# Sums of weight blocks on VectorE instead of GpSimd, and one ScalarE copy placed later, in a hybrid decoder trunk

## What is computed

```
u = rmsnorm(h) * valid
(a_q, a_f, a_i, a_g, b_qkv, ..., c_gk, c_g, gate_logits) = split(u @ w_in)
y_a = hgrn2(...); y_b = gated_deltanet(...); y_c = gla(...)
gates = sigmoid(gate_logits)                       # 3 x 1024 columns of w_in
merged = sum over the three of gates * (y @ w_branch)
h = h + merged @ w_out
h = h + hier_moe(rmsnorm(h))                       # 32 experts, top 2
out = rmsnorm(h)
```

## Time and profile before

| | |
|---|---|
| time, median of 3 runs | 1096.6 us (1095.65 to 1100.54) |
| the profiled execution's own time | 1095.69 us |
| its span in the trace | 1093.3 us |
| mean granted TensorE clock | 0.981 |
| busy: PE | 1035.0 us (95%) |
| busy: DVE | 528.0 us (48%) |
| busy: ACT | 309.3 us (28%) |
| busy: POOL | 137.4 us (13%) |

### The profile page before, as it was taken

The page is one execution under the profiler, slowest core; times in us unless marked ns, Lnnn a source line. Parts: engine busy times, 40 slices in busy tenths (PEclk is TensorE's granted clock), DMA queues, the critical chain, the costliest instruction groups (busy, mean ns, idle before and its releaser), DMA issues. The chain is left out here.

```text
span 1093.3 us, 20473 instructions
## 1 busy us (share of the span) xinstructions
PE 1035.0 (95%) x8841; PEld 697.7 (64%) x8841; DVE 528.0 (48%) x1026; ACT 309.3 (28%) x573; POOL 137.4 (13%) x121
## 2 busy tenths in 40 slices
PE   9999999998998998998999999999998999878897
PEld 8676676876776776776756556444456665535454
DVE  5766566658458457458454454423235322111114
ACT  3454535343343343243333033010110111001013
POOL 4220202022022022022000000000001222211110
PEclk9999999999999998999999999999999999989899
DMA  9222212240241230331212211154937999999976
GB/s 275 59 59 59 76 43 77 64 97 24 75 82 28 72 82 20 79 74 32 76 44 74 59 58 60 58 201 156 350 136 284 409 414 414 415 417 414 416 318 240
DMA packets 111964, 174.72 MB, mean 160 GB/s; under 512 B 9011, under 2 KB 87100, under 8 KB 103554
## 3 DMA queue, kind: packets, MB, share of 16 engines
q1 hardware_dynamic: 99010, 134.93, 35.7%
q10 hardware_dynamic: 7136, 27.33, 6.3%
q0 software_dynamic: 5728, 11.14, 3.8%
HBM read 169.16 MB, written 12.60 MB: 166 GB/s over the span
## 5 line engine op out<-in xcount | busy, mean ns | idle before, releaser
L791 PE MATMUL ps<-arena 128*128 128x256 f32 x672 | 168.6, 395 | 0.0
L791 PEld LDWEIGHTS ps<-arena 128*128 128x128 f32 x672 | 123.4, 193 | 17.1
L1465 DVE TENSOR_TENSOR arena<-arena 128x256 f32<-128x256 f32 (+6 forms) x198 | 103.5, 565 | 60.0 <-ACT arena L1261 37.0
L824 PE MATMUL ps<-arena 128*128 128x512 f32 x288 | 128.2, 595 | 1.2 <-DVE arena L1804 1.2
L821 PE MATMUL ps<-arena 128*128 128x264 f32 x400 | 123.1, 389 | 0.8 <-DVE gates L1563 0.8
L822 PE MATMUL ps<-arena 128*128 128x264 f32 x400 | 121.7, 386 | 0.0
L2289 PE MATMUL ps<-arena,gates 128*64 128x256 f32 (+1 forms) x1088 | 106.4, 354 | 15.9 <-DMA arena<-in_expert_w_up 15.8
L2289 PEld LDWEIGHTS ps<-arena,gates 128*64 128x64 f32 x1088 | 73.6, 144 | 55.1 <-DMA arena<-in_expert_w_up 24.1
L824 PEld LDWEIGHTS ps<-arena 128*128 128x128 f32 x288 | 53.6, 190 | 62.3 <-issue 61.8
L815 PE MATMUL ps<-yT,arena 128*128 128x512 f32 x192 | 84.8, 596 | 2.1 <-DVE gates L1563 1.4
L822 PEld LDWEIGHTS ps<-arena 128*128 128x128 f32 x400 | 76.0, 190 | 13.0
(11 more groups left out here) (373 smaller groups left out, 1394.5 us busy)
## 6 DMA issues: line engine op xcount, KB each, us to landing
arena<-in_w_in SPq DMA_DIRECT2D x68, 512.0 KB, 3.9
arena<-in_expert_w_gate SPq DMA_DIRECT2D x27, 1024.0 KB
arena<-in_expert_w_up SPq DMA_DIRECT2D x27, 1024.0 KB
arena<-in_expert_w_down ACTq DMA_DIRECT2D x16, 1024.0 KB, 33.4
arena<-in_w_branch SPq DMA_DIRECT2D x12, 512.0 KB, 4.0
arena<-in_expert_w_down SPq DMA_DIRECT2D x6, 1024.0 KB, 17.2
C<-in_expert_w_gate SPq DMA_DIRECT2D x5, 1024.0 KB
gates<-in_expert_w_up SPq DMA_DIRECT2D x5, 1024.0 KB
```

What stands on the lines that cost most here:

```text
L791: mm = t.matmul(dst, wt[:, k, :], rhs[:, k, :], start=(k == 0), stop=(k == KH - 1))
L824: mm = t.matmul(dst, wt, uT[:, k, META:], start=(k == 0), stop=(k == KD - 1))
L1465: v.tensor_tensor(out_, a_, b2, op).then_inc(*q.did(name))
```

## The change

The twelve quadruples of sums go from GpSimd's list to VectorE's, each sum at a place of its own in the round: A's S1 and S2 at level 1 behind the gate product, S4 and S3 at level 2; B's S1, S2 and S4 between `min` and `kn`, and S3 between `less` and `unit` of q; C's S1 at level 1 of B's round, S2 at level 2, S4 and S3 at level 4. The arithmetic and the waits are the same; S3 now waits for S4, and the semaphore `pair_weights` is counted by VectorE. GpSimd keeps the four token mixes of the setup and its transfers. Apart from that, `keep_product` of B stands behind the softplus of the values on ScalarE instead of ahead of it. TensorE's list is the same instruction for instruction.

```diff
-            def mix_weights(stage, r):
-                n, p = pair_block(stage, r), pair_no(stage, r)
...
-                g.tensor_tensor(s1, second[:, 0:KH], second[:, KH:], ALU.add).then_inc(*pair_pool.did(f"S1.{p}"))
...
             mix_tokens()
-            for r in range(A_R - 1):
-                mix_weights("a", r)
...
-                mix_weights("b", r)
-                mix_weights("c", r)
...
                 a.activation(b_n, pair(4), ACT.Copy).then_inc(*b_act.did(f"N.{r}"))
-                keep_product("b", r)
                 a.wait_ge(*b_dve.after(f"v3.{r}"))
                 softplus(b_act, ("abv", "ev", "lv"), r, b_vb[:, 0:TOK], b_s[:, 0:TOK])
+                keep_product("b", r)
                 a.wait_ge(*b_dve.after(f"tv.{r}"))
...
+            def mix_weights(name, stage, r):
+
+                n, p = pair_block(stage, r), pair_no(stage, r)
+                first, second = ring[:, n % RING, :, :], ring[:, (n + 1) % RING, :, :]
+                s1, s2, s4 = (mixed_w[:, m] for m in range(3))
+                if name == "S1":
+                    for m in (n, n + 1):
+                        v.wait_ge(sem(f"block_loaded{m % RING}"), (m // RING + 1) * 16)
+                if name in ("S2", "S4"):
+                    v.wait_ge(*pair_mix.after({"S2": "S1", "S4": "S2"}[name] + f".{p}"))
+                if p and name != "S3":
+                    v.wait_ge(*pair_pe.after({"S1": "P5", "S2": "P6", "S4": "P3"}[name] + f".{p - 1}"))
+                if name == "S3":
+                    v.wait_ge(*pair_mix.after(f"S4.{p}"))
...
+                v.tensor_tensor(out_, a_, b2, op).then_inc(*pair_mix.did(f"{name}.{p}"))
...
                         tt(a_dve, f"g.{r}", a_g, real(0), a_sg)
+                        mix_weights("S1", "a", r)
+                        mix_weights("S2", "a", r)
+                    if l == 2:
+                        mix_weights("S4", "a", r)
+                        mix_weights("S3", "a", r)
...
+                mix_weights("S1", "b", r)
+                mix_weights("S2", "b", r)
+                mix_weights("S4", "b", r)
                 v.wait_ge(*b_act.after(f"rik.{r}"))
                 tt(b_dve, f"kn.{r}", b_kf, b_kf, b_em)
...
                 less("q", b_nw[:, 0:TOK], cq, b_nw[:, 0:TOK], r)
+                mix_weights("S3", "b", r)
                 unit("q", b_qf, cq, b_nw, r)
```

More of the change, by code:

```diff
@@ L540, in hybrid_trunk @@
                       each(C_R - 1, c_finish_names()))
-        pair_pool = Order("pair_weights", [f"{n}.{p}" for p in range(PAIRS) for n in ("S1", "S2", "S4", "S3")])
+        pair_mix = Order("pair_weights", [f"{n}.{p}" for p in range(PAIRS) for n in ("S1", "S2", "S4", "S3")])
         pair_pe = Order("pair_products", [f"{n}.{p}" for p in range(PAIRS) for n in ("P1", "P5", "P6", "P3")])
@@ L684, in mixers_gpsimd @@
             g.wait_ge(sem("rows_sent"), 16)
-            mix_weights("a", A_R - 1)
             rv = rows_dram.rearrange("(t h) (k p) -> k h t p", h=B_R, k=2)
@@ L763, in pair_step @@
                             t.wait_ge(*tokens_mixed.after("T4"))
-                        t.wait_ge(*pair_pool.after(f"S1.{p}"))
+                        t.wait_ge(*pair_mix.after(f"S1.{p}"))
                         if stage == "c":
@@ L769, in pair_step @@
                     if name == "P6":
-                        t.wait_ge(*pair_pool.after(f"S2.{p}"))
+                        t.wait_ge(*pair_mix.after(f"S2.{p}"))
                         t.wait_ge(*pair_copy.after(f"P1.{p}"))
                     if name == "P3":
-                        t.wait_ge(*pair_pool.after(f"S4.{p}"))
+                        t.wait_ge(*pair_mix.after(f"S4.{p}"))
                         if stage == "c":
@@ L778, in pair_step @@
                     if name == "P7":
-                        t.wait_ge(*pair_pool.after(f"S3.{p}"))
+                        t.wait_ge(*pair_mix.after(f"S3.{p}"))
                         t.wait_ge(*pair_sum.after(f"U2.{p}"))
@@ L1523, in c_finish @@
                     tt(c_dve, f"y_{s}.{r}", yT[:, 8 + 2 * r + s, :], c_zz[s], c_g[s])
+            def mix_weights(name, stage, r):
[11 more added lines that the diff above has]
+                    v.wait_ge(*pair_mix.after(f"S4.{p}"))
+                out_, a_, b2, op = {"S1": (s1, second[:, 0:KH], second[:, KH:], ALU.add), "S2": (s2, s1, first[:, 0:KH], ALU.subtract),
+                                    "S4": (s4, first[:, KH:], s2, ALU.subtract),
+                                    "S3": (second[:, 0:KH], first[:, 0:KH], second[:, 0:KH], ALU.subtract)}[name]
+                v.tensor_tensor(out_, a_, b2, op).then_inc(*pair_mix.did(f"{name}.{p}"))
             def gate_second(stage, r):
```

21 lines of the change are left out of this document (6 added, 15 removed).

## The result

The changed kernel takes 1081.68 us (median; 1079.12 to 1082.65) against 1096.12 us for the kernel before in the same comparison: ratio 0.9856, 95% interval 0.9824 to 0.9888. The prediction was 1080, with a range of 1076 to 1086. The profiled execution took 1080.85 us, with a span of 1079.0 us against 1093.3 before.

A forecast was written before the change was run, and what follows sets the result against it. TensorE, 95% busy, was the bound, so other engines count only where it waits, in stage B. 10.7 + 0.9 + 4.9 - 0.1 = 16.4 us gave 1079.3, put at 1080; range 1077 to 1082, with two rivals 1076 to 1086.

The forecast's parts named there:

- The chain to `vT` and `Z1`: Stage B: shorter `Da`, `vm`, `vr` and an earlier logarithm start `Z1` 2.67 us earlier per round, 10.7 us in four.
- rival (3): GpSimd isn't the cause of the long `Da`, `vm`, `vr`; only the copy's 2.4 us remain, 1094 us; chance 0.05.
- The spare time at `vT`: Stage B: the wait of 2.51 us at `vT` goes, with 0.3 us to spare.
- Round 0: Round 0 of B: `less` of k gets 0.94 us shorter, which fits into the waits at `ssk` and `KK`: 0.9 us.
- no cost, no gain: GpSimd's transfers of decay and beta rows keep their place with nothing ahead of them, so the time does not change.
- The clock: Stage B: without the long wait the granted clock does not fall in rounds 0 to 2, 4.9 us, between 0 and 4.9.
- The pause ahead of `kn`: Stage B: three sums of 2.18 us fill VectorE's pause of 2.25 us; 0.1 us lost in all, up to 0.4.
- A's sums: Levels 1 and 2 of A: four sums, about 2.9 us, end 1.3 us before TensorE asks at level 3; no wait.
- C's sums and S3: Stage B: C's sums fit where VectorE waits in the levels, S3's 0.60 us in a pause of 0.71; no cost.
- (1): The clock falls all the same, or at another place; 11.5 us are won, 1085 us; chance 0.10.
- (4): The pauses are too short, since a sum takes VectorE 1.47 to 1.58 us; slower, 1103 us; chance 0.04.
- (2): A wait at P6 or `vT` takes the old one's place; 2 to 4 us less won, 1082 to 1084 us; chance 0.12.

The follow-up runs named there:

- e1: The kernel before with only ScalarE's copy of P1 moved behind the softplus of the values in B, sums left on GpSimd: 1089.77 us, 0.9933 of before.
- e10: The changed kernel with four more VectorE operations between `tv` and `Da` in each round of B: 1096.36 us, 0.9989 of before.
- e7: The changed kernel with ScalarE's root of the keys moved ahead of the two exponentials in B, sums unmoved: 1079.15 us.
- e3: The kernel before with the copy moved and GpSimd's sums for C's pair waiting for VectorE's `qg` of the round: 1081.45 us, 0.9861 of before.
- e2: The changed kernel with the copy of P1 moved back ahead of the softplus, sums on VectorE: 1085.23 us, 0.9898 of before.
- e6: The changed kernel with B's S1, S2 and S4 moved into earlier pauses of VectorE, ScalarE's order unchanged: 1080.58 us.
- e5: The changed kernel with both the keys' root ahead of the exponentials and B's S1, S2, S4 in earlier VectorE pauses: 1072.58 us, 0.9782 of before.
- e11: The changed kernel with two more VectorE operations between `tv` and `Da` in each round of B: 1085.82 us.
- e12: The kernel before with each of GpSimd's S1 and S2 cut into four operations of 128 columns, at the same place: 1088.86 us, 0.9914 of before.
- e4: The changed kernel with one more VectorE operation of a sum's shape ahead of `kn` in each round of B: 1082.99 us.

## Why the prediction was right

*The chain to `vT` and `Z1`* (10.7 us): measured 4 x 2.67 = 10.7. Each link came out as the prediction had it: `Da` 0.82, `vm` and `vr` 0.78, the logarithm 0.6 us earlier with `tv` behind it, no wait of `vT`, none of P6. That it was added up in a straight line was right because both parts act at once: the terms 0.6 and 2.1 us add up only because no operation on the chain meets a sum of GpSimd any more. e1 shows that the same terms do not hold one by one; the prediction's rival (3) priced the copy alone at 0.6 us a round, and it is worth 1.18.

*The spare time at `vT`* was put at 0.3 us and is 0.14: `vr` ends at 417.46 and `vT` starts at 417.60. `Z1` waits 0.60 us where the prediction allowed 0.4 at most. TensorE begins `vT` 0.16 us ahead of the end that the trace models for the group in front of it (414.14 + 3.62 = 417.76), and I had reckoned with that end. It cost nothing in the sum, since `Z1`'s start was worked out from `Db`.

*Round 0* (0.9 us): this term was mis-sized. `less` of k came down from 1.65 to 0.71 us and `ssk`'s wait of 0.52 went, but only 0.44 us arrived, and `KK` waits 1.38 there. The step that failed is "the 0.94 us fits into these two waits": on its way VectorE meets something that was hidden behind it before, the decay rows, which GpSimd had asked for and which the prediction called "no cost, no gain". Round 0 of B, VectorE:

```profile
236.59 0.71 DVE L1687 SCALAR_TENSOR_TENSOR arena<-arena 128x528 f32<-128x528 f32 x1 [1.81 <-ACT arena L1228]
...
242.55 0.82 DVE L1441 TENSOR_TENSOR arena<-arena,bcol 128x640 f32<-128x640 f32 x1 [0.69 <-DMA arena<-token_rows]
```

*The clock* (4.9 us): measured 5.26 + 5.37 + 6.86 + 4.31 before against 4 x 4.30 after, 4.6. The two short falls, scaled by the missing clock to 1.2 us each, were 0.96 and 1.07. Another 0.4 us came from two later levels, 439.20 to 443.73 in round 2 (4.53 us, 4.31 after) and 515.82 to 520.32 in round 3 (4.50 us, 4.32 after). The granted clock is 1.00 there, so they are not the clock's, and the prediction had no term for them. The prediction held the waits for the cause without having shown it; e10 shows it.

*The pause ahead of `kn`* (0.1 us lost): nothing was lost, and 0.20 us remain. The three sums take 2.13 to 2.14 us from start to end and hold VectorE for 2.06 us (399.48 to 401.54 in e7), where the prediction had 2.18: a sum that waits for its predecessor starts some 0.05 us behind its end, (2.14 - 3 x 0.68) / 2, and not 0.11, which is what `kb` still shows behind `kn` (402.23 + 0.83 to 403.17). The Trainium skill (VectorE: DVE Perf Modes, "The DRAIN you can't avoid") has a semaphore cost nothing extra; an estimate by it, with three sums of 0.68 us that overlap by 0.08, is 1.9 us for what took 2.14.

*A's sums* (nothing): right, with 1.8 us to spare at level 3 and not 1.3, since two sums take 1.41 us and not 1.45, and some of them fell into idle time that the prediction had charged in full. *C's sums and S3*: no wait of TensorE for any of them.

The sum was 16.4 and B gave 16.1: 10.7 + 0.4 + 4.6 + 0.4. That the two are so close is partly luck: round 0 and the clock gave 0.8 us less than forecast, and 0.4 us that nobody had reckoned with and the 0.1 us at `kn` made up for most of it. The median came out 1.7 us above 1080. A late start such as the 1.4 us of the profiled execution would be enough for that, but the runs do not show that it is the cause in all four; they range over 3.5 us.

Of the rivals, (1) is refuted for these waits and (3) by e3; (4) by the row of 0.68 us a sum. (2) would have needed 0.14 us more at `vT`: e2, which keeps the copy in its old place, comes close to that rival, with 0.42 us of waiting a round.

## What to carry to other kernels

When an operation takes twice as long at one place as its twin does at another, look at what GpSimd does when it starts, and move either of the two, or cut GpSimd's instruction into short ones; where the work sits matters more than which engine has it (e3 ties with the change at the cost of one wait). Behind such a fix look for the place where two chains end together: moving the sums or the root ahead of `kn` singly gave 0.0 and 0.3 us a round (e6, e7), and moving both gave 2.0 (e5, rounds 1 and 3, which have no stops: 76.07 and 77.17 us in place of 78.05 and 79.14), and a wait that is hidden today, as the decay rows were, is where the next microsecond stops. Count a wait of TensorE with the clock's fall behind it: in e10, 9.8 us of waiting cost 15.6.

## What the runs showed of the hardware

- VectorE's operations with two SBUF inputs and GpSimd's sums hold each other up by whole instructions: the second ends 0.5 to 0.7 us (VectorE, 512 to 640 columns) or 1.12 to 1.14 us (GpSimd, 512) behind the first. An operation with an input in PSUM was not held (0.68 us in e1).
- Granted clock, by the waits of TensorE ahead of it in a round: 2.29 and 0.60 us, four falls in four rounds (e10); 2.51 with 0 to 0.60, three (before); 0.85 and 1.07, three (e1); 0.97 and 0.60, two (e11); 0.88 and 0.68, none (e12, where one fall stood behind 2.03 us at `KK`); 0.42 and 0.60, none (e2); 1.34 at `KK` alone with 0.60 at `Z1`, 15 us apart, none (e4). Each fall costs 1.0 to 2.6 us. That equal rounds of one kernel differ (e1, e11, before) is not explained.
- TensorE stops at times for 0.15 to 1.25 us among its small products with nothing to wait for ("issue"), in seven of the twelve kernels tried. Not explained.
